# A head's modulation item: eight slices multiplied and added up on VectorE, four products of ones on TensorE

## The reference

```
mod = (silu(c) @ w_ada + b_ada)                     # c is one row of 1024; w_ada is 1024 x 6144
shift1, scale1, gate1, shift2, scale2, gate2 = split(mod, 6)
h = rms_norm(x) * (1 + scale1) + shift1
z = h @ w_in                                        # conv, latent q and kv, branch gates
merged = sigmoid(g_conv) * conv_mixer(z) + sigmoid(g_mla) * attention(z)   # 8 heads of 128
x = x + gate1 * (merged @ w_o)
h2 = rms_norm(x) * (1 + scale2) + shift2
x = x + gate2 * mixture_of_32_experts(h2)
```

## Time and profile before

| | |
|---|---|
| Median of 3 runs | 553.23 us (552.34 to 556.12) |
| The profiled execution's own time | 554.89 us |
| Its span in the profile | 553.1 us |
| TensorE matmul busy | 507.1 us (92%) |
| VectorE busy | 185.5 us (34%) |
| ScalarE busy | 147.4 us (27%) |
| GpSimd busy | 152.9 us (28%) |
| HBM read | 160.35 MB, 292 GB/s over the span |
| Granted TensorE clock, mean | 0.97 |

### The profile page before, as it was taken

One profiled execution on the slowest core, in us unless ns is written; L12 is line 12 of the kernel. 1 busy time (PEld: TensorE's weight loads), 2 busy tenths in 40 slices (PEclk: granted clock), 3 DMA queues, 4 the chain that ended last, 5 costly groups with the idle time before them and its releaser, 6 DMA issues.

```text
span 553.1 us, 14782 instructions
## 1 busy us (share of the span) xinstructions
PE 507.1 (92%) x6173; PEld 398.1 (72%) x6174; DVE 185.5 (34%) x561; ACT 147.4 (27%) x275; POOL 152.9 (28%) x195
## 2 busy tenths in 40 slices
PE   2769999999999999999999598999899899899895
PEld 2558888888888888888888485666666666666663
DVE  1620245242424242324231643333233233233233
ACT  2100113232323232313130521333323323323321
POOL 0000001000000101010100002777667667667662
PEclk9969999999999999999999868999999999999999
DMA  8993505468687764543437950978999999999982
GB/s 348 436 423 146 223 1 232 158 256 348 262 355 293 311 238 153 224 153 152 153 153 262 410 239 2 367 318 353 421 441 425 430 426 433 439 432 427 426 363 77
DMA packets 10257, 161.89 MB, mean 293 GB/s; under 512 B 1136, under 2 KB 2416, under 8 KB 2544
## 3 DMA queue, kind: packets, MB, share of 16 engines
q1 hardware_dynamic: 10224, 161.40, 70.9%
HBM read 160.35 MB, written 1.05 MB: 292 GB/s over the span
## 4 chain that ended last, share of the span: by engine, by line
PE 82%; DMA 11%; DVE 3%; issue 2%; ACT 1%; SPq 1%; DVEq 0%; ACTq 0%
PE ps L450 78%; DMA wex<-in_ex 6%; DMA wex<-in_ada 4%; PE ps L707 1%; PE ps L681 1%; ACT act L423 1%; PE ps L682 1%; DVE xT L996 1%; DVE act L788 0%; DVE work L890 0%; SPq L244 0%; PE ps L606 0%; PE ps L615 0%; PE ps L614 0%; PE ps L616 0%
## 5 line engine op out<-in xcount | busy, mean ns | idle before, releaser
L450 PE MATMUL ps<-act,wmix 128*128 128x256 f32 x864 | 195.8, 384 | 3.4 <-DVE act L788 3.4
L450 PEld LDWEIGHTS ps<-act,wmix 128*128 128x128 f32 x864 | 163.7, 192 | 27.2 <-DMA wmix<-in_lat 3.6
L337 POOL TENSOR_SCALAR work<-trig,work 128x256 f32<-128x256 f32 x70 | 64.9, 936 | 71.8 <-issue 62.5
L450 PE MATMUL ps<-wex,work 128*32 128x128 f32 (+1 forms) x1840 | 70.7, 301 | 10.9 <-issue 9.0
L323 POOL TENSOR_TENSOR work<-work,trig 64x256 f32<-64x256 f32 x8 | 5.8, 720 | 262.6 <-ACT work L388 161.0
L450 PE MATMUL ps<-work 32*128 32x256 f32 (+6 forms) x864 | 72.8, 375 | 0.5 <-ACT work L444 0.5
L450 PEld LDWEIGHTS ps<-wex,work 128*32 128x32 f32 x1840 | 50.3, 112 | 28.6 <-issue 13.6
L450 PEld LDWEIGHTS ps<-work 32*128 32x128 f32 (+3 forms) x864 | 47.5, 168 | 13.2 <-issue 3.3
L441 ACT ACT_TABLE_LOAD x35 | 44.9, 1283 | 4.1 <-issue 0.8
L341 POOL TENSOR_TENSOR work<-work,trig 128x512 f32<-128x512 f32 x35 | 44.6, 1275 | 0.0
L450 PE MATMUL ps<-act,work 128*32 128x256 f32 (+1 forms) x704 | 42.4, 360 | 0.9 <-issue 0.9
(11 more groups left out here) (175 smaller groups left out, 429.4 us busy)
## 6 DMA issues: line engine op xcount, KB each, us to landing
wex<-in_ex SPq DMA_DIRECT2D x20, 3072.0 KB, 18.7
wex<-in_ada SPq DMA_DIRECT2D x12, 2048.0 KB, 11.3
wmix<-in_ex SPq DMA_DIRECT2D x8, 3072.0 KB, 19.7
wmix<-in_mix_even SPq DMA_DIRECT2D x4, 3200.0 KB, 10.6
wmix<-in_mix_odd SPq DMA_DIRECT2D x4, 3008.0 KB, 10.7
work<-in_ex SPq DMA_DIRECT2D x4, 2048.0 KB, 20.3
wmix<-in_wo SPq DMA_DIRECT2D x2, 2048.0 KB, 7.5
act<-in_ex SPq DMA_DIRECT2D x4, 1024.0 KB, 15.7
```

Source lines behind the costliest of these rows:

```text
L337: nc.gpsimd.tensor_scalar(comb_both[:, rows], slot_row[:, rows], lane_now, None, ALU.is_equal).then_inc(comb_half, 1)
L450: return nc.tensor.matmul(out, lhsT, rhs, start=start, stop=stop, **kw)
```

## The change

The eight items of the head loop are no longer computed by 32 matmuls each. VectorE multiplies slice k (128x512) by the column `c_rep[:, k, 0:1]` and adds it to `ada_sum`, one instruction for each k (the first a `tensor_scalar`, seven `scalar_tensor_tensor`), in two parts: slices 0 to 4 behind `conv_gated(j)` at the end of head j-1 (for item 0, ahead of the loop), and slices 5 to 7 in head j, behind `merge(j-1)` and, in even heads, between L847 and L849. TensorE then sums over partitions with four matmuls, 128x32 ones against each quarter of `ada_sum`. `ada_sum` lies in place 3 of `wex`, behind `ada_rows`. The reload of `ada_beside` waits for VectorE's last step of the item (`ada_summed`) in place of TensorE's last matmul (`ada_done`). VectorE has the wait for the item's landing (`ada_landed`) that TensorE had.

```diff
+        ada_sum = wex[:, OWN - 1, GU_COLS + P:GU_COLS + P + ADA_TILES * P]
...
             def beside_load(j):
-                sp.wait_ge(ada_done, 4 + j)
+                if j == 0:
+                    sp.wait_ge(ada_done, 4)
+                else:
+                    sp.wait_ge(ada_summed, j)
                 sp.dma_start(ada_beside, ada_d[4 + j]).then_inc(ada_landed[3], 16)
...
-                pe.wait_ge(ada_landed[3], 16 * h + 32)
-                ada_item(ada_beside, ps[:, 0, 0:P]).then_inc(ada_done, 1)
+                pe.wait_ge(ada_summed, h + 1)
+                for q in range(4):
+                    last = mm(ps[q * WIN:(q + 1) * WIN, 0, 0:P], ones[:, 0:WIN], ada_sum[:, q * P:(q + 1) * P], True, True)
+                last.then_inc(ada_done, 1)
...
+            def ada_steps(j, steps):
+
+                w = ada_beside.rearrange("p (k c) -> p k c", k=KT)
+                if steps[0] == 0:
+                    dve.wait_ge(ada_landed[3], 16 * j + 32)
+                    dve.wait_ge(ada_done, 4 + j)
+                for k in steps:
+                    if k == 0:
+                        link(v.tensor_scalar(ada_sum, w[:, k, :], c_rep[:, k, 0:1], None, ALU.mult))
+                    elif k < KT - 1:
+                        link(v.scalar_tensor_tensor(ada_sum, w[:, k, :], c_rep[:, k, 0:1], ada_sum, ALU.mult, ALU.add))
+                    else:
+                        v.scalar_tensor_tensor(ada_sum, w[:, k, :], c_rep[:, k, 0:1], ada_sum, ALU.mult, ALU.add).then_inc(ada_summed, 1)
+
             conv_taps(0)
             conv_gated(0)
+            ada_steps(0, range(0, 5))
...
                 if h % 2 == 0:
                     dve.wait_ge(qx_ready, h // 2 + 1)
                     link(v.tensor_tensor(q_r, q_x, cos_t, ALU.mult))
+                    ada_steps(h, range(5, KT))
                     dve.wait_ge(swap_ready, h // 2 + 1)
...
+                if h % 2 == 1:
+                    ada_steps(h, range(5, KT))
                 dve.wait_ge(rk_sqrt, h + 1)
...
                     conv_gated(h + 1)
+                    ada_steps(h + 1, range(0, 5))
```

More of the change, by code:

```diff
@@ L221, in block_kernel @@
         ada_copied, ada_turned = sem("ada_copied"), sem("ada_turned")
+        ada_summed = sem("ada_summed")
         mod_ready = sem("mod_ready")
```

## The result

| | before | changed kernel |
|---|---|---|
| Median | 553.86 us (552.34 to 556.12, 4 runs) | 578.89 us (568.47 to 584.99, 4 runs) |
| Ratio | | 1.0289 (95%: 1.0251 to 1.0326) |
| Profiled execution | 554.89 us, span 553.1 | 584.86 us, span 583.0 |

The change makes the kernel slower by 2.9%, outside the range given. The times of the changed kernel scatter, and the ratio is taken from the two of its four executions that lie within 1.5% of its shortest, 568.47 and 572.93; the medians of all four stand 4.5% apart. The profiled execution is among the long ones. Its loss of 30 us is the one whose places are read here; the shorter ones left no trace.

What follows compares the result with a forecast made beforehand. TensorE was taken as the bound (82% of the chain, no gap in the head loop). Three longer heads (2.0 + 3.1 + 2.0) less 5 x 1.65 gave -1.2 us; 2.1 for the clock made +0.9: 554.2 us by the median, range 548 to 560.

Steps and rivals of the forecast that it cites:

- The experts' stage moves as a whole: Experts' stage behind the head loop: shifts without changing length, since events of TensorE issue all its loads; no term for it.
- What goes from TensorE: Head loop: item's 1.89 us replaced by four products of ones; gain 1.65 us per head, 0.84 at the upper bound.
- The four products: TensorE's matmuls of ones on the summed item, each head: 8 records, 0.24 us, upper bound 1.05.
- VectorE's slices: VectorE's item steps: 0.75 us each plus 0.04 link; 3.7 us for slices 0 to 4, 2.4 for 5 to 7.
- the free heads: Five items with no expert ahead in the queue: in time for VectorE, each giving its full 1.65 us.
- The item's landing: DMA queue, head 1: item behind an expert still lands at V(1) + 22.9 despite earlier issue; VectorE stands still 8 us.
- The three bound heads: Heads 1 to 3, late item delays the merge: V to V 29.6, 29.8, 29.6 us; 2.0, 3.1, 2.0 longer.
- The clock's part: Lower TensorE clock behind the three gaps: 1.3 us at v products plus 0.8 behind the last; bounds 0 to 6.1.
- The rival "as meant": Head loop: item there in time, all eight heads give 1.65 us, 540.0 us; chance 0.12.
- The slow rivals: Head loop: clock falls in all three gaps, 558.2 or 562.2 us, chance 0.07; VectorE's steps double, 565.3, chance 0.05.

Runs made afterwards that it cites:

- e7: e3 with 64 tiny matmuls (256 instructions, a whole block) at the start of TensorE's program; 563.66 us, ratio 1.0154.
- e3: Changed kernel with one swap on SP: the head's modulation item issued ahead of the expert in heads 1 to 3; 569.50 us, ratio 1.0240.
- e1: Changed kernel with 128 instructions (256 waits already met) at the start of TensorE's program; 555.97 us, ratio 1.0026.
- e4: Changed kernel with both the swap on SP and the 128 instructions at the start of TensorE's program; 540.23 us, ratio 0.9743.

## Why the prediction was wrong

It was wrong in one step, a sentence at the end of the sum: "The experts' stage moves as a whole: all its loads are issued by events of TensorE." That is true of the loads. It left out that TensorE's own instructions are loaded too, and that 896 fewer of them ahead of a loop move the loop against its blocks. The loop's ways back stood at nothing in the sum. The runs show in its place a loss of 28 us in the changed kernel's profiled execution of that stage (227.1 us for 199.0), of 24 to 31 in e7 and e3, and 1.0213 as the ratio of such a shift alone in the kernel before, with 16.6 us lost there. With the loop back in a good place, the changed kernel takes 555.97 us against the forecast 554.2, so the rest of the sum came out within 2 us.

By its own steps, otherwise:
- *What goes from TensorE*: 1.52 to 1.53 us for each head (27.56 to 26.03 and 26.69 to 25.17 in e3), 1.65 forecast. The four products hold the next tile back 0.36 us, not 0.24.
- *VectorE's slices*: 0.751 us each for 0.75 forecast, with no wait for an item in the free heads.
- *The item's landing* is the same wherever it is issued behind an expert: V + 23.3 for 22.9 forecast in head 1, with three waits of VectorE for an item. Right, and e3 shows the cause.
- *The three bound heads*: 31.0, 30.3, 31.2 measured, 29.6, 29.8, 29.6 forecast before the clock. In e1, with gaps of 3.6, 2.4 and 2.8 us, 30.8, 29.6, 29.6. The clock's part was larger than the 2.1 forecast, though within its bounds: 1.0 us at the v products of two heads, and 1.7 behind the last gap (26.88 us from V(4) to V(5), 25.17 in e3), 3.7 in all. The head loop lost 4.7 us in the profiled execution of the changed kernel and 1.7 in e1's (206.5 us for 204.8), 0.9 forecast.
- *The rival "as meant"* gave 540.0 us for an item in time and the loop where it was. e4 is that case with the queue's order changed: 540.23. That they agree so closely is luck: of the 14.7 us between the profiled executions the head loop gave 12.2, where the rival had 13.2, and the rest stood in no sum.
- *The slow rivals* had their causes in the head loop. None was what made the kernel slower: e1, with the same head loop, is 1.0026 of the kernel before.

## What to carry to other kernels

An edit that changes the number of instructions ahead of a long loop can move its time by several per cent, though the loop is untouched (here by 2 to 9%): compare the gap on the loop's way back and the packets of the instruction queue before you judge the edit, and if they changed, shift the code by half a block with instructions in an idle stretch and time it again. A wait moved from the engine that needed the data late to one that needs it early must be checked against the landing time, not the issue time, where the queue ahead is full. And an edit with two opposite effects needs a run for each: e3 alone would have said that the order of the queue does not matter.

## What the runs showed of the hardware

- A way back over this loop costs 1.4 us well placed and 7.2 to 8.2 us badly placed beside a full DMA queue, 4.9 us beside a nearly idle one. Positions 128 and 192 instructions on are good, 0, 64 and 256 bad.
- Behind a bad way back nine packets of 16 KB arrive on the instruction queue before the next way back, behind a good one none.
- The loop is seven windows of 115 matmuls and 115 loads, with some 12 waits, register instructions and branches each: TensorE carried out about 1690 instructions from 434.6 to 476.0 in the kernel before, 6.6 blocks. The second break, behind some 120 instructions of the loop, gives an estimate of where the loop lies: it starts about 136 instructions into a block in e3 and with 256, 8 with 128, 72 with 192, 200 with 64. From there 1690 instructions touch eight, seven, seven and eight blocks. The good and bad positions thus fit a store of eight blocks, the 2048 instructions that the Trainium skill ("Runtime: NRT & Kernel Launch", "Instruction fetch mechanics") gives TensorE, if a block from behind the loop can take the place of one of the loop's before the way back. That eight are too many is argued from the positions, not shown.
- In the changed kernel, idle gaps of TensorE of 3.8 and 4.0 us had brought the granted clock to 0.50 when work came back; behind one of 3.1 us it stood at 1.00.
